# Three projection pieces moved from the front into expert block 0, and one row buffer joining the ring of buffers 17 groups later

## What is computed

```
proj = rmsnorm(h) @ w_in                  # q, k, v of two groups of heads
o_a = stick_breaking_attention(qa, ka, va)           # 8 heads, strictly causal
o_b = sliding_window_sink_attention(qb, kb, vb)      # 8 q heads, 2 kv heads, rotary
h = h + concat(rmsnorm(o_a), rmsnorm(o_b)) @ w_out
# PEER: for each token and each of 8 heads the 16 best of 128*128 experts
u, v = expert_u[idx], expert_v[idx]                  # 128 rows per token
h = h + sum_k softmax(top_s)[k] * gelu(u[k] . t) * v[k]
out = rmsnorm(h)
```

## Time and profile before

| what | us |
|---|---|
| median of 3 runs | 2919.9 |
| lowest and highest | 2914.4 and 2925.72 |
| profiled execution, its own time | 2919.07 |
| span of that execution | 2917.0 |

### The profile page before, as it was taken

One profiled execution on the slowest core, in us unless ns is written; L12 is line 12 of the kernel. 1 busy time (PEld: TensorE's weight loads), 2 busy tenths in 40 slices (PEclk: granted clock), 3 DMA queues, 4 the chain that ended last, 5 costly groups with the idle time before them and its releaser, 6 DMA issues.

```text
span 2917.0 us, 30220 instructions
## 1 busy us (share of the span) xinstructions
PE 2214.7 (76%) x9182; PEld 950.5 (33%) x9182; DVE 2184.8 (75%) x5506; ACT 1145.3 (39%) x2673; POOL 1316.1 (45%) x1126
## 2 busy tenths in 40 slices
PE   9989888788887988867887777867755775665556
PEld 7564532345333453313322332212311231111111
DVE  4189887786777868679786888779776987668555
ACT  3523377433563335633575326733212331121111
POOL 0024355444554435544565445644444444444442
PEclk9999999899999999979998898988877898767778
DMA  8279999999999999999999999999999999999997
GB/s 320 95 303 409 386 410 418 401 412 380 412 397 419 411 398 414 366 419 419 419 415 417 421 413 409 408 410 418 421 420 422 420 404 421 418 421 411 422 421 321
DMA packets 198096, 1155.22 MB, mean 396 GB/s; under 512 B 23648, under 2 KB 53792, under 8 KB 66480
## 3 DMA queue, kind: packets, MB, share of 16 engines
q0 software_dynamic: 147456, 1073.81, 89.6%
q1 hardware_dynamic: 50480, 79.50, 7.5%
HBM read 1138.21 MB, written 15.01 MB: 395 GB/s over the span
## 4 chain that ended last, share of the span: by engine, by line
DMA 33%; PE 29%; DVE 23%; ACT 8%; issue 4%; POOL 2%; SPq 0%; ACTq 0%; DVEq 0%; POOLq 0%
DMA r_uv<-in_experts,r_wk 31%; PE ps L1868 13%; DVE r_uv L1430 11%; PE ps L1540 4%; PE ps L1786 2%; ACT r_uv L1016 2%; PE ps L1764 2%; PE ps L1534 2%; ACT L1013 2%; POOL r_uv L756 1%; DVE r_wk L1201 1%; DVE r_wk L1199 1%; DVE r_wk L1202 1%; PE ps L1556 1%; DMA r_wk<-lq_dram 1%
## 5 line engine op out<-in xcount | busy, mean ns | idle before, releaser
L756 POOL DMA_INDIRECT r_uv<-in_experts,r_wk x1024 | 1212.8, 1184 | 1406.1 <-PE ps L1868 1191.8
L1868 PE MATMUL ps<-r_uv 128*64 128x512 f32 x4096 | 1234.5, 735 | 668.6 <-ACT r_uv L1016 655.8
L1430 DVE CUSTOM_DVE_ANT_0 r_uv<-r_uv,hnrep 128x1024 f32<-128x1024 f32 x1024 | 1253.8, 1240 | 548.4 <-DMA r_uv<-in_experts,r_wk 539.4
L1868 PEld LDWEIGHTS ps<-r_uv 128*64 128x64 f32 x4096 | 291.1, 157 | 1409.7 <-ACT r_uv L1016 943.9
L1013 ACT ACTIVATE r_wk<-r_wk 128x2 f32<-128x2 f32 x512 | 103.9, 203 | 1446.5 <-DVE r_wk L1430 1445.0
L1016 ACT ACTIVATE r_uv<-gid,r_wk 128x64 f32<-128x64 f32 x684 | 200.7, 340 | 11.6 <-ACT r_wk L1013 0.3
L1013 ACT ACT_TABLE_LOAD x138 | 177.1, 1283 | 2.5
L777 ACT ACT_TABLE_LOAD x117 | 150.1, 1283 | 8.1 <-PE ps L1744 3.7
L1540 PE MATMUL ps<-r_uv,stream_chunk 128*128 128x256 f32 x560 | 134.1, 394 | 3.8 <-DMA stream_chunk<-in_w_chunks 3.8
L1786 PEld LDWEIGHTS ps<-r_wk,r_wq 128*128 128x128 f32 x1024 | 119.6, 193 | 37.0 <-issue 36.5
L1786 PE MATMUL ps<-r_wk,r_wq 128*128 128x128 f32 x1024 | 128.7, 280 | 0.3 <-ACT r_wk L933 0.3
(11 more groups left out here) (181 smaller groups left out, 2217.1 us busy)
## 6 DMA issues: line engine op xcount, KB each, us to landing
r_uv<-in_experts,r_wk POOLq DMA_INDIRECT x1024, 13.5
stream_chunk<-in_w_chunks SPq DMA_DIRECT2D x30, 512.0 KB, 8.0
r_wk<-lkv_dram SPq DMA_DIRECT2D x72, 128.0 KB, 7.5
r_uv<-in_x SPq DMA_DIRECT2D x8, 512.0 KB, 10.3
r_wo<-in_w_chunks SPq DMA_DIRECT2D x8, 512.0 KB, 11.1
r_wk<-in_x SPq DMA_DIRECT2D x8, 512.0 KB, 8.2
r_wo<-in_w_out SPq DMA_DIRECT2D x8, 512.0 KB, 9.5
r_wq<-in_w_query SPq DMA_DIRECT2D x8, 512.0 KB, 6.8
```

Of the source, the lines that this page charges most:

```text
L756: g.indirect_dma_start(uv[:, SLOT[G], :], None, experts, bass.IndirectOffsetOnAxis(idx[b % 2][:, k:k + 1], 0)).then_inc(rows_in[SLOT[G]], 16)
L1430: v.tensor_tensor_reduce(uv[:, slot, 0:D], uv[:, slot, 0:D], hnrep[:, k % GRP, :], 1.0, 0.0, ALU.mult, ALU.add, actv[:, k:k + 1]).then_inc ...
L1868: last = t_.matmul(ps[HALF * j:HALF * j + HALF, i, :], uv[:, slot, 0:HALF], uv[:, slot, D + 512 * i:D + 512 * i + 512], start=n == 0, stop ...
```

## The change

`NH`, the number of pieces that the front does, goes from 16 to 13, and the front's steps 14, 17 and 20 lose their pieces. All 18 pieces of tokens 256 to 511 are now in block 0: piece 13 takes group 0, where piece 16 was, and so on, and three new places follow behind groups 52, 55 and 58. Which weights a place reads therefore shifts by three pieces; from block 1 on nothing moves. Buffer 1 joins the ring at group 60 instead of 43. PE's waits that belonged to front pieces are renamed or dropped, and SP waits for finished stores before it loads the first late unit of pair 3.

```diff
-NH = NF + 3
-SPARE = NF + 11
+NH = NF
+SPARE = NF + 8
...
-FRONT_AT = list(range(13)) + [14, 17, 20]
+FRONT_AT = list(range(13))
...
-STREAM_GROUPS = ([0, 1, 2, 4, 6, 7, 8, 9, 12, 20, 22, 24, 33, 36, 39]
+STREAM_GROUPS = ([0, 1, 2, 4, 6, 7, 8, 9, 12, 20, 22, 24, 33, 36, 39, 52, 55, 58]
...
-PIECE_BANK = [i % 2 for i in range(NF)] + [0, 1, 1] + [7] * (NP - NH)
+PIECE_BANK = [i % 2 for i in range(NF)] + [7] * (NP - NH)
...
-ONE_MORE, NARROW, WIDE = 43, 56, STREAM_BLOCKS * NG
+ONE_MORE, NARROW, WIDE = 60, 56, STREAM_BLOCKS * NG
...
+                    if b == 0 and i == PAIRS - 1 and units[u - 1][0] != i:
+                        stored(pieces_by(at))
...
-                if i == NF + 1:
-
-                    gate(pe, "pe", ob_added, 1)
...
-                        pe.wait_ge(proj_kept, NF + 1)
+                        pe.wait_ge(proj_kept, NF)
...
-                    pe.wait_ge(proj_kept, NF + 3)
+                    pe.wait_ge(proj_kept, NF)
```

## The result

| kernel | us, median (lowest to highest) | runs |
|---|---|---|
| before | 2919.9 (2914.4 to 2929.89) | 5 |
| after | 2937.95 (2926.85 to 2943.58) | 5 |

The ratio is 1.0055, 95% interval 1.0034 to 1.0076: slower by about 16 us, where 2 us were forecast. A ratio here is always the recorded one, which is not the plain quotient of the two medians (the two differ by up to 0.0016). The profiled execution of after took 2926.85 us, 7.8 more than that of before.

The account below looks back on a forecast made before the run. It held the kernel bound by DMA bytes from group 0 on, and before that by the front's dependent chain. 2919.07 - 6.35 (front gain) + 4.7 (bytes) + 4.5 (ring) = 2921.9 us; range 2911 to 2934.

Parts of the forecast that it names:

- The ring: Group 60's first gather waits for piece 30, leaving the DMA engines without gathers: 4.5 us lost, bounds 0 and 8.2.
- its sign in POOL's row: Sign of a right forecast: POOL waits 8 us or more for L1539 ahead of group 60.
- SP: SP's load order and new store wait around groups 52 to 58: 0 us, upper bound 2.8 for a late chunk.
- Rival B: At group 58, chunk 30 behind `xs_dram` delays piece 30, buffer 1 and POOL: 11 us, total 2928.4; chance 0.15.
- The clock: Slow clock after the front's new PE gaps: one 3 us loss at even odds, 1.5 us; bounds 0 and 6.
- rival C: Both new front gaps are followed by slow stretches: front gain only 1.85 us, total 2926.4; chance 0.14.
- Pieces 13 to 15: Removing front steps 14, 17 and 20's pieces brings the first gather forward 7.85 us before clock loss; upper bound 8.55.
- Moved bytes: Three chunk loads and three stores, 1.97 MB, move to block 0's end: 4.7 us cost, lower bound 1.5.

Follow-up runs that it names:

- experiment 5: The kernel after with buffer 1 joining the ring at group 62 instead of 60: 2923.91 us, ratio 1.0005.
- experiment 4: The kernel before with buffer 1 joining the ring at group 60 instead of 43, nothing else changed: 2921.76 us, ratio 1.0003.
- early pieces: The kernel after with its last three pieces behind groups 42, 45, 48 and the join at 52: 2919.18 us, ratio 1.0001; run again, 2926.26 us, 1.0010.
- The version with early pieces and 19 products: After with pieces behind 42, 45, 48, join at 52, 19 unused TensorE products and padded ScalarE: 2916.73 us, ratio 0.9984 to before.

## Why the prediction was wrong

The sum forecast +2.9 us on the profiled execution. Term by term:

- *The ring*, 4.5 us: this is the step that failed. Groups 58 to 60 lost 10.6, 10.9, 8.6 and 10.0 us in the four profiles with late pieces and the join at 60, more than even the upper bound of 8.2, and experiment 5 gave 7.9 of it back by one number. The mechanism was as described (POOL waits for piece 30, all gathers behind it), and so was its sign in POOL's row. The size was wrong because I took the issue of group 59's gathers, 502.7 and 504 us, from the trace of before, 7.9 us behind the start of group 55's products. Six buffers alone leave that as it is (7.8 us in experiment 4). With the late pieces they left 13.2 to 15.0 us behind it, in after at 518.19 and 519.43. The products of group 56, behind which they wait, began there 11.0 us behind group 55's, not 5.7: piece 29 took 3.69 us, PE then stood 3.23 us for SP's small load, and the products themselves took 3.68 us, not 1.94. Group 59's gathers are the last work in the queue before the join. They did not lie 15 us ahead of the hole but at its edge, and the queue ran dry. The sentence "four groups lay between piece and gather there; now it is two" named the right quantity, but no price followed from it.
- *SP*, which I put at nothing: wrong too, and part of the same delay. The last late unit's two loads of 8 KB now stand behind the chunk of 512 KB and the store of 128 KB that the place at group 52 brings. They were issued 3.6 to 5.0 us ahead of group 55's products, as in the kernels without late pieces (3.6 to 4.4), but they landed 13.3 to 13.6 us after their issue in the two profiles that tell it, 2.6 us behind that store; in the three without late pieces that tell it, it is 6.6 to 7.1. PE waited for them 2.1 to 3.2 us in all five profiles with late pieces, 1.2 us at most in the others. How much of the 10 us hangs on it is open: no kernel has these two loads ahead of the chunk and the join at 60.
- *Rival B*'s price, 11 us, was near, by luck; its cause was not. The last chunk did stand behind `xs_dram`: in two profiles it landed 3.5 and 3.7 us behind it, 13.8 and 15.2 us after its own issue, where I had 8.0. But it came in time: piece 30 starts at 526.94, right behind group 58.
- *The clock*, one loss at even odds, 1.5 us: both new gaps lost it, in every profile without the added products. The front's gain is 59.35 - 54.95 = 4.4 us like for like, and 62.6 - 61.1 = 1.5 between the two first profiles, since behind the old gap the slow stretch lasts longer in after (10.2 us at 0.50 against 6.8). That piece 13's dense products had ended it sooner in before is my reading; no run tests it. Forecast 6.35; rival C said 1.85.
- *Pieces 13 to 15*, 7.85 us without the clock: with every gap filled the front is 59.4 - 52.0 = 7.4 us shorter. Nearly right.
- *Moved bytes*, 4.7 us: six profiles with early pieces lost 3.2 to 4.6 us between groups 40 and 54; of two with the old places one lost 0.7 and one gained 0.9. In the late places the loss of 3.1 to 4.0 us between groups 54 and 59 is of the size of two pieces' bytes. Right, or a little high.
- *Not foreseen*: ScalarE's stop, about 5 us.

With the measured sizes the sum is 2919.07 - 1.5 + 5 + 4.7 + 10.6 = 2937.9 with the stop, and 2919.07 - 4.4 + 4.7 + 10.9 = 2930.3 without it; the medians of after were 1.0055 and 1.0038 times before, or 2936 and 2931 on 2919.9. These sums use differences from single traces, so their agreement to a microsecond is chance; after's own profiled execution took 2926.85, far below the first. The range failed with the ring: I gave a time above 2934 only 0.07, because I held the wait at the join to 8.2 us.

The version with early pieces and 19 products is the best that ran (0.9984), but its interval holds 1: no kernel is shown to beat before.

## What to carry over

Where a wait is put at the join of a ring, work out when, in the changed kernel, the last gathers ahead of the waiting one are issued: they, not those in the trace of before, are what the queue still has to do. Two groups between the last piece and the join were too few here (10 us), with four groups the hole was gone. For that time, follow every wait of the engine that frees the buffers, a small load behind a large one in the same queue too: put at nothing here, it held TensorE for 3 us. And when dense work is taken out of a chain on TensorE, price the clock behind each gap that it leaves: here it took back about 3 of 7.4 us at the least. In the two profiles with 19 unused products it was all there again; with 13 alone, in two profiles, the front was no shorter, since the slow stretch behind the old gap was there.

## What the runs showed of the hardware

- Idle gaps of 0.76 and 2.42 us on TensorE were each followed by a granted clock of 0.50 in six profiles of six (L1763 5.40 to 6.48 us instead of 3.70, the 20 products of L1785 3.54 to 3.82 instead of 2.47), and filled with products of 128 columns in none of four. A gap of 1.43 us was followed by it in 5 of 11, filled in none of 3.
- Two loads of 8 KB behind one of 512 KB and a store of 128 KB in SP's queue landed 13.3 to 13.6 us after issue, in two profiles; without these ahead of them 6.6 to 7.1 us.
- ScalarE's stop: idle 6.7 to 7.0 us at the same instruction in 9 of 14 profiles, ending 11.6 to 11.8 us after the first gather of the kernel, with no releaser in the profile.
- A gain in the front need not last: in one execution with before's own code up to group 42, a front that was 2.9 us earlier at group 2 was 0.2 us earlier at group 40.
